# An attention-like mixing stage: maxima spread by TensorE, deeper slots, one mask per head

## What is computed

```python
d = where(mask, b[t] - b[s] + i[s], -inf)
mt = maximum(inter, max(d))
s  = (q @ k.T) * exp(d - mt)
num, den = s @ v, sum(s)
h = num / maximum(abs(den), exp(-mt))
```

## Time and profile before

| what | value |
|---|---|
| median of 3 runs | 3360.03 us (3357.69 to 3368.77) |
| profiled execution | 3349.2 us, span 3347.0 us |
| TensorE, VectorE, ScalarE, GpSimd busy | 92%, 71%, 54%, 16% of the span |
| the mixing stage | 243.7 to 376.8 us of the span |

### The profile page before, as it was taken

One profiled execution on the slowest core, in us unless ns is written; L12 is line 12 of the kernel. 1 busy time (PEld: TensorE's weight loads), 2 busy tenths in 40 slices (PEclk: granted clock), 3 DMA queues, 4 the chain that ended last, 5 costly groups with the idle time before them and its releaser, 6 DMA issues. The chain is left out here.

```text
span 3347.0 us, 67501 instructions
## 1 busy us (share of the span) xinstructions
PE 3063.0 (92%) x27056; PEld 2572.3 (77%) x27056; DVE 2390.1 (71%) x3547; ACT 1820.2 (54%) x3016; POOL 543.3 (16%) x566
## 2 busy tenths in 40 slices
PE   6996889999797988879999999998999999999997
PEld 4773568878672877759986898856988988998896
DVE  5857663468747445577866778554899999999996
ACT  2523333232314665535445444774878878878875
POOL 0005124321100221018423111430000000000000
PEclk8998989999898999989989999998999999999998
DMA  6537224436221000048642788402999999999994
GB/s 221 167 103 24 88 83 148 136 134 231 85 67 25 5 5 4 4 164 270 255 154 68 278 319 298 124 27 76 358 362 361 377 356 364 373 354 366 362 366 180
DMA packets 288465, 647.73 MB, mean 194 GB/s; under 512 B 24605, under 2 KB 144521, under 8 KB 288201
## 3 DMA queue, kind: packets, MB, share of 16 engines
q1 hardware_dynamic: 267321, 568.39, 49.7%
q0 software_dynamic: 20160, 73.41, 6.0%
q10 hardware_dynamic: 720, 2.23, 0.2%
HBM read 640.82 MB, written 1.05 MB: 192 GB/s over the span
## 5 line engine op out<-in xcount | busy, mean ns | idle before, releaser
L4850 DVE TENSOR_TENSOR weights_lo<-raw_ring,weights_hi 128x896 fp32r<-128x896 f32 (+1 forms) x376 | 413.1, 1125 | 50.3 <-ACT weights_hi L4803 40.8
L4803 ACT ACTIVATE weights_hi<-raw_ring 128x896 fp32r<-128x896 f32 (+1 forms) x376 | 366.9, 986 | 90.1 <-PE bank_pair L4773 87.9
L4773 PE MATMUL bank_pair<-weights_hi,expert_x_hi 128*128 128x448 f32 x1024 | 294.1, 368 | 5.1 <-DVE weights_lo L4850 5.1
L4773 PE MATMUL bank_pair<-weights_hi,expert_x_lo 128*128 128x448 f32 x1024 | 291.9, 366 | 0.0
L4773 PE MATMUL bank_pair<-weights_lo,expert_x_hi 128*128 128x448 f32 x1024 | 291.9, 366 | 0.0
L4850 DVE TENSOR_TENSOR weights_lo<-H,weights_hi 128x896 fp32r<-128x896 f32 (+1 forms) x240 | 264.0, 1131 | 22.7 <-ACT weights_hi L4803 14.6
L4803 ACT ACTIVATE weights_hi<-H 128x896 fp32r<-128x896 f32 (+1 forms) x240 | 236.8, 990 | 68.0 <-PE bank_pair L4773 68.0
L2682 DVE SCALAR_TENSOR_TENSOR conv<-bank_pair,vec,conv 128x189 f32<-128x189 f32 (+3 forms) x396 | 138.5, 428 | 147.2 <-ACT conv L2642 147.2
L4773 PEld LDWEIGHTS bank_pair<-weights_hi,expert_x_hi 128*128 128x128 f32 x1024 | 190.0, 189 | 20.7 <-issue 5.0
L4773 PEld LDWEIGHTS bank_pair<-weights_lo,expert_x_hi 128*128 128x128 f32 x1024 | 192.9, 188 | 15.8
L4773 PEld LDWEIGHTS bank_pair<-weights_hi,expert_x_lo 128*128 128x128 f32 x1024 | 192.9, 188 | 15.7
(11 more groups left out here) (827 smaller groups left out, 8336.8 us busy)
## 6 DMA issues: line engine op xcount, KB each, us to landing
raw_ring<-in_moe_w_gate SPq DMA_DIRECT2D x72, 896.0 KB, 6.8
raw_ring<-in_moe_w_up SPq DMA_DIRECT2D x64, 896.0 KB, 7.2
ring_up<-in_ffn_w_up SPq DMA_DIRECT2D x110, 512.0 KB, 4.5
raw_ring<-in_moe_w_down SPq DMA_DIRECT2D x48, 1024.0 KB, 7.5
mod_ring_ada<-in_w_ada POOLq DMA_DIRECT2D x84, 512.0 KB, 6.5
H<-in_moe_w_up SPq DMA_DIRECT2D x48, 896.0 KB, 7.3
ring_down<-in_ffn_w_down SPq DMA_DIRECT2D x66, 512.0 KB, 6.5
H<-in_moe_w_down SPq DMA_DIRECT2D x32, 1024.0 KB, 7.5
```

What stands on the lines that cost most here:

```text
L4773: ins = nc.tensor.matmul(banks[half][:, 0:b - a], x, w[:, a:b], start=start and i == 0, stop=stop and i == 2)
L4803: nc.scalar.activation(hi[:, u % CUTS, 0:n].bitcast(F32R), raw_part(u), ACT.Copy).then_inc(cut.sem, 1)
L4850: nc.vector.tensor_tensor(lo[:, u % CUTS, 0:n].bitcast(F32R), raw_part(u)[:, 0:n], hi[:, u % CUTS, 0:n], ALU.subtract).then_inc(parted.sem, 1)
```

## The change

- The maxima of the first two heads come by TensorE: the unit column of a head, broadcast as weights, times the four rows of `rowmax`, into the TURN banks, copied to `maxb` by ScalarE. The other six heads still come by DMA, with four buffers in place of two.
- `mask` is one instruction per head over four blocks (128x512), in place of four of 128x128; from the third head on it is issued after the third product of the head before.
- Three weight slots in place of two, five key slots in place of two.
- The first pair's shift moves from GpSimd to VectorE, between the first two masks. ScalarE exponentiates the first pair before any weights, and the others three steps ahead, after the step's first item, in place of two steps ahead and in front of it.
- `scale` does half a pair at a time: queries two steps ahead, keys one step ahead. `add_up` follows the step's first product.
- The items are spread over one step more (`LAST = 19`).
- In PV the copies to `Y` are done head by head, and two "inv" spreads stand behind the first PV step, two between the halves of the second; the norms of the second direction stand at VectorE's end.
- `num` moves to a part of `H`; `near` and `far` take freed slots of `qk`.

```diff
-    ITEMS, LAST = 8 * 4, 18
+    ITEMS, LAST, KEYS, WEIGHTS = 8 * 4, 19, 5, 3
...
-        return u % 2 if j == 0 else 2 + (3 * u + j - 1) % 2
+        return u % 2 if j == 0 else 2 + (3 * u + j - 1) % self.KEYS
...
+        masked, weight, pt = sb("masked", [P, 2, TT]), sb("weight", [P, M.WEIGHTS, TT]), sb("pt", [P, 2 + M.KEYS, TT])
+        den, num, maxb, every = sb("den", [P, TT]), st.H[:, 4:8], sb("maxb", [P, 4, TT]), sb("every", [4, P])
+        qk, att = sb("qk", [P, 3, 2, 2, TT]), st.H[:, 0:4]
+        near, far = (qk[:, i].rearrange("p x c t -> p x (c t)") for i in (0, 1))
...
-            for i in M.pairs[0:2]:
-                shift(pool, nc.gpsimd, i)
+            for e in (1, 2):
+                shift(pool, nc.gpsimd, M.pairs[e])
             for i in range(M.STEPS):
-                if M.opens(i + 4) and i + 4 not in M.pairs[0:2]:
+                if M.opens(i + 4) and M.pair_no(i + 4) > 2:
...
+                if u < 2:
+                    continue
+                if u >= 4:
+                    sp.wait_ge(masked_ready.sem, masked_ready.at(u - 3))
+                    sp.wait_ge(weights.sem, weights.at(4 * u - 12))
+                sp.dma_start(maxb[:, u % 4], ev.rowmax[d][h:h + 1, :].unsqueeze(1).to_broadcast([1, P, TT])).then_inc(max_landed[u % 4].sem, 16)
...
+                if kind == "max":
+                    d, h = M.heads[i]
+                    nc.tensor.matmul(bank, st.C("ident")[0:4, h:h + 1].to_broadcast([4, P]), ev.rowmax[d][:], start=True, stop=True).then_inc(spread.sem, 1)
...
+                        ins.then_inc(valued.sem, 1)
+                        if (c, hh) in ((0, 1), (1, 0)):
+                            for h in (0, 1):
+                                use_turn("inv", ML_HEADS + 2 * c + h)
...
+            for u in (0, 1):
+                use_turn("max", u)
             use_turn("score", 0)
...
+                    for hh in (0, 1):
+                        act.wait_ge(valued.sem, valued.at(2 * c + hh + 1))
+                        nc.scalar.activation(st.Y[:, 4 + 2 * c + hh], PAIR[i % 2][:, hh * TT:(hh + 1) * TT], ACT.Copy)
...
+                if m >= M.WEIGHTS:
+                    act.wait_ge(pt_ready.sem, pt_ready.at(m - M.WEIGHTS + 1))
+                w = weight[:, m % M.WEIGHTS]
...
+            for u in (0, 1):
+                act.wait_ge(spread.sem, spread.at(u + 1))
+                nc.scalar.activation(maxb[:, u], turn_bank("max", u), ACT.Copy).then_inc(max_copied.sem, 1)
+            exp(M.pairs[0])
             for i in range(M.STEPS):
-                if M.opens(i + 2):
-                    exp(i + 2)
...
+                    if m == M.items_of(i)[0] and M.opens(i + 3):
+                        exp(i + 3)
...
-            def scale(i):
+            def scale(i, x):
...
+                to, of = qk[:, e % 3, x], ev.gqk[:, 2 * x:2 * x + 2]
+                if l == FAR:
+                    to = to.rearrange("p c (d t) -> p c d t", d=2)
+                    of = of[:, :, 0 if x else CTX:CTX if x else TT].unsqueeze(2).to_broadcast([P, 2, 2, CTX])
+                ins = nc.vector.tensor_tensor(to, of, to, ALU.mult)
+                if x:
+                    ins.then_inc(scaled.sem, 1)
...
-            def mask(m):
-                u, s, _ = M.items[m]
+            def mask(u):
                 d, h = M.heads[u]
-                dve.wait_ge(max_landed[u % 2].sem, max_landed[u % 2].at(16 * (u // 2) + 16))
-                if m >= 2:
-                    dve.wait_ge(weights.sem, weights.at(m - 1))
-                nc.vector.scalar_tensor_tensor(masked[:, m % 2], maxb[:, u % 2, s * P:(s + 1) * P], -1.0, st.C("neg_after" if d else "neg_before"),
-                                               ALU.mult, ALU.add).then_inc(masked_ready.sem, 1)
+                if u < 2:
+                    dve.wait_ge(max_copied.sem, max_copied.at(u + 1))
+                else:
+                    landed = max_landed[u % 4]
+                    dve.wait_ge(landed.sem, landed.at(32 if u >= 6 else 16))
+                    dve.wait_ge(weights.sem, weights.at(4 * u - 4))
+                blocks = lambda x: x.rearrange("p (b t) -> p b t", t=P)
+                side = st.C("neg_after" if d else "neg_before").unsqueeze(1).to_broadcast([P, 4, P])
+                nc.vector.scalar_tensor_tensor(blocks(masked[:, u % 2]), blocks(maxb[:, u % 4]), -1.0, side, ALU.mult, ALU.add).then_inc(masked_ready.sem, 1)
...
             mask(0)
+            shift(dve, nc.vector, M.pairs[0])
+            mask(1)
             for i in range(M.STEPS):
-                if M.opens(i + 1):
-                    scale(i + 1)
-                for m in M.items_of(i):
-                    if m + 1 < M.ITEMS:
-                        mask(m + 1)
+                l, c = M.gla[i]
+                if M.opens(i + 2 - c):
+                    scale(i + 2 - c, c)
+                for n, m in enumerate(M.items_of(i)):
                     product(m)
+                    if m % 4 == 2 and 1 < m // 4 + 1 < len(M.heads):
+                        mask(m // 4 + 1)
                     if m == 19:
                         invert(0)
                     if 20 <= m < 20 + ML_HEADS:
                         norm(m - 20)
-                if i == M.LAST + 1:
+                    if n == 0:
+                        add_up(i)
+                if i == M.LAST:
                     invert(1)
-                add_up(i)
-                if i >= M.STEPS - 2:
-                    for h in (0, 1):
-                        norm(ML_HEADS + 2 * (i - M.STEPS + 2) + h)
+            for h in range(ML_HEADS):
+                norm(ML_HEADS + h)
```

More of the change, by code:

```diff
@@ L2097, in __init__ @@
         self.uses, self.at = [], {}
+        self.use("max", 0)
+        self.use("max", 1)
         self.use("score", 0)
@@ L2157, in even_mix_stage @@
         sb = lambda name, shape: core.sb(name, shape, ctx=ctx)
[L2158 to L2165, removed]
+        masked, weight, pt = sb("masked", [P, 2, TT]), sb("weight", [P, M.WEIGHTS, TT]), sb("pt", [P, 2 + M.KEYS, TT])
+        den, num, maxb, every = sb("den", [P, TT]), st.H[:, 4:8], sb("maxb", [P, 4, TT]), sb("every", [4, P])
+        qk, att = sb("qk", [P, 3, 2, 2, TT]), st.H[:, 0:4]
+        near, far = (qk[:, i].rearrange("p x c t -> p x (c t)") for i in (0, 1))
+        assert [(l - 1) % 3 for l in (NEAR - 1, NEAR, FAR)] == [0, 1, 2]
+        first_shifted, shifted, exps, scaled, scored, summed, moved, valued = (
+            core.counter("gla_" + n) for n in ("first_shifted", "shifted", "exps", "scaled", "scored", "summed", "moved", "valued"))
+        spread, max_copied, scores, masked_ready, weights, pt_ready, pt_used, num_copied, keys_added, den_summed = (
+            core.counter("ml_" + n) for n in ("spread", "max_copied", "scores", "masked_ready", "weights", "pt_ready", "pt_used", "num_copied", "keys_added", "den_summed"))
         floor_ready, floored, den_copied, inverted, inv_ready, normed, every_ready = (
             core.counter("ml_" + n) for n in ("floor_ready", "floored", "den_copied", "inverted", "inv_ready", "normed", "every_ready"))
-        max_landed = [core.counter(f"ml_max_landed{i}") for i in (0, 1)]
+        max_landed = [core.counter(f"ml_max_landed{i}") for i in range(4)]
         PAIR = [core.psum[0], core.psum[1]]
@@ L2242, in wait_turn @@
                     before, n = M.uses[at - 2]
-                    taken = {"score": pt_ready, "floor": floored, "inv": normed}[before]
+                    taken = {"max": max_copied, "score": pt_ready, "floor": floored, "inv": normed}[before]
                     pe.wait_ge(taken.sem, taken.at(n + 1))
@@ L2248, in use_turn @@
                 bank = turn_bank(kind, i)
-                if kind == "score":
+                if kind == "max":
+                    d, h = M.heads[i]
+                    nc.tensor.matmul(bank, st.C("ident")[0:4, h:h + 1].to_broadcast([4, P]), ev.rowmax[d][:], start=True, stop=True).then_inc(spread.sem, 1)
+                elif kind == "score":
                     u, s, runs = M.items[i]
@@ L2439, in product @@
                         dve.wait_ge(den_summed.sem, den_summed.at(u - 1))
[L2440 to L2441 removed]
+                elif k >= M.KEYS:
+                    n = k - M.KEYS
                     dve.wait_ge(pt_used.sem, pt_used.at(4 * (n // 3) + n % 3 + 2))
```

43 lines of the change are left out of this document (11 added, 32 removed).

## The result

The changed kernel takes 3337.89 us, median of 6 executions (3328.52 to 3348.04); the kernel before, beside it, 3358.86 (6, 3349.34 to 3368.77). The medians differ by 21.0 us; the ratio is 0.9933 with an interval of 0.9915 to 0.9951, which is 16 to 29 us less. The forecast was 3343 and a gain of 17.1. The profiled execution of the changed kernel took 3328.52 us, its span is 3326.7, so against the 3347.0 of before the profile shows 20.3 us.

What follows compares the result with a forecast made beforehand. The mixing stage was taken as limited by engines waiting for each other, VectorE nearest to a bound in the middle. Terms 3.0 + 2.6 + 9.0 + 2.5 + 1.5 - 2.7 + 1.2 gave 17.1 us, so 3343; range 3335 to 3355.

Steps and rivals of the forecast that it cites:

- the price of turns: VectorE instructions with two SBUF inputs and GpSimd ones reading SBUF exclude each other; old masks waited 0.25 us each.
- Start: Stage's start: TensorE's spread replaces the wait for a transfer of first maxima; gain 3.0 us, bounds 6.1 to 2.0.
- Masks: On VectorE, 32 masks become 8 of four times the width, 16.9 us become 7.9; gain 9.0.
- Split scales: On VectorE, 18 scale halves issued singly wait for more turns than pairs; loss 2.7 us, bounds 0 and 16.
- Slots and scores: VectorE's waits: held key slots gain 2.5 us (bounds 0 and 4.5), TensorE's scores 1.5 (bounds 0 and 5.5).
- Later transfers: VectorE's later waits for transfers of maxima go with two more buffers, issued two heads ahead; gain 2.6 us.
- End: Stage's end: a half-size copy of 0.60 us follows TensorE's last work, instead of four norm instructions; gain 1.2 us.
- moved turns: Rival, chance 0.20: whatever VectorE issues next pays the turns, masks gain only 3.5 us; total gain 7.6, 3352.
- TensorE's bound: Rival, chance 0.15: all VectorE waits vanish and steps run as fast as TensorE works; stage 108.2 us, 3335.
- the late shift: Rival, chance 0.07: GpSimd's shift comes too late for the earlier exponential and scale, VectorE stands still; 3372 us.

Runs made afterwards that it cites:

- the second profile: The changed kernel run once more, unchanged: stage 113.8 us, against 115.4 in its first profile.
- the last experiment: Changed kernel with the first pair's shift on GpSimd, denominator products one item later and their first copy behind the weights: 3324.08 us, ratio 0.9903.
- the experiment that forced it: Changed kernel with GpSimd adding its keys before it shifts a pair in each step: stage 5.3 to 6.9 us longer.

## Why the prediction was right, and where it was not

Sign and size came out: a gain of 17.1 was forecast for the stage, 17.3 measured, and 18.9 by the second profile. Of the mechanism, the price of turns came out; the slots, the scores and the reason given for the transfers did not. By steps:

- *Start*, forecast 3.0, measured 2.7. Right for its reason: turns were taken every time, four subtractions of 6.3 us in all where 6.9 was the bound. What I did not do was to price the same start with the shift left on GpSimd; the run shows 3.2 us more. Nor did I see that the other bound, 2.8, could be had: in front of the first mask the same four took 2.7.
- *Masks*, forecast 8 at 0.99 us, 7.9 in all; measured 0.989 and 7.9. The price in turns holds (the narrow masks show it). But the step from "9.0 us of VectorE" to "9.0 us of the stage" is not shown: on the kernel before, masks and buffers gave 3.9, and four narrow masks in the changed kernel cost 4.5 to 6.1.
- *Split scales*, forecast 27.0, measured 26.9. As a price right; the whole pairs shortened neither VectorE's total nor the stage: the masks then took 9.3 us in place of 7.9, and item 17 came 2.9 later.
- *Slots and scores*, 2.5 and 1.5. These steps failed as terms. Waits for held slots went, but the run with two slots has them and is no longer; waits for scores stayed at 5.6 and, in the second profile, 4.6 (5.5 in the earlier trace rows), and a stall of 4.1 that I did not foresee came in. What the runs show in their place is one effect, slots or order, worth 7.0 to 8.6 us of the stage in one profile, of which either is mostly enough. That the order would carry any of it stands nowhere in the sum.
- *Later transfers*, 2.6: gone, as forecast, but not by the buffers that the term was put down to. With four buffers and all eight heads by transfer, on the kernel before and on the changed one, later masks waited 5.3 and 6.9 us. The step that failed is that each transfer has two heads' time: they land one behind the other. What took the waits away is that the first two heads no longer stand in that queue.
- *The middle as a whole*: masks, scales, slots, scores and transfers sum to 12.9 in the forecast and 12.1 in the trace, 8.0 from VectorE's busy time and 4.1 from its waits. The sum was better than its parts, in part by luck: terms for slots and scores stood in for an effect of slots and order that the sum did not have, and the stall of item 18, which it did not have either, took some of it back.
- *End*, forecast 1.2, measured 2.5. The last lines are as foreseen, ScalarE's half copy behind the norm:

```profile
355.71 0.69 DVE L2484 TENSOR_TENSOR Y<-Y,H 128x512 f32<-128x512 f32 x1
...
357.17 0.60 ACT L2363 ACTIVATE Y<-bank_pair 128x512 f32<-128x512 f32 x1 [3.77 <-PE bank_pair L2312]
```

  TensorE's idle time in that stretch fell by 1.3 (22.51 - 20.60 to 20.00 - 19.36), which is the forecast's term; the other 1.2 is work, 114 matmuls instead of 127, that was done before the last product. I had read the end as if the same work were left there.

Of the rivals, moved turns would have shown masks over 12 us; TensorE's bound was 7 us off in this kernel, and the last experiment has its length without being bound by TensorE; the late shift did not occur, and the experiment that forced it lost 5.3 to 6.9.

## What to carry to other kernels

Where two engines take turns, price an instruction by the turn it waits for as well as by its length, and move work across only after pricing it at both places: merged masks gained, the shift moved behind the first mask lost 3. Prices of single instructions can be summed for an engine, but not for a stage: a saved wait may be saved twice, and a stall further on can take up what a part costs. Before a part is called useless, look how far the kernel had come ahead of the next stall, and undo it together with the part that could be doing its work. An "issue" wait with nothing named is worth following through every queue; here it led to a version whose stage is shorter than both.

## What the hardware showed that was not expected

A burst pays more than the same instructions spread out: 32 narrow masks took 532 ns each one by one among other work and 741 in bursts of four, with GpSimd about as busy (61.5 of 109 us there, 58.4 of 95 here); that is one profile of each. Which engine waits depends on where an instruction stands: four subtractions on VectorE took 6.3 us behind the first mask and 2.7 as its first instructions, where GpSimd's one beside them took 3.53 instead of 1.04. And two executions of one binary differed by 1.6 us in one stage although their order was the same: behind the same stall TensorE's granted clock was 0.90 in one and 0.99 in the other, and it ran the floor's spread in 2.07 us and 1.36.
